# Router on the residual rows, two prefetched parts behind the first gather, and GpSimd adding the returned rows of two tiles, in a hybrid encoder with a mixture of experts

## The chip, the cores and the metric

The kernel runs on one core of a Trainium2 chip. The metric is the device time of one execution in microseconds (us). PE is TensorE, DVE is VectorE, ACT is ScalarE, POOL is GpSimd, and SP is SyncE, which here only issues DMAs.

## The reference

One encoder layer on 512 tokens of 1024 float32 values: a token mixer (windowed attention and gated linear attention, merged and added to the input), then a mixture of experts, then a last RMS norm. The change touches what follows the token mixer.

```python
hn = rms_norm(x, norm_ffn[l])
x = x + hier_moe(hn, ...)
return rms_norm(x, norm_final)

# hier_moe, for each token
g_logits = xt @ w_rg + b_rg                      # 4 groups, the best is taken
e_logits = xt @ w_re + b_re                      # 32 experts, the 2 best of that group are taken
top_w = softmax(top_v) * g_w                     # the weights of the 2 experts
h = silu(xt @ w_gate[e]) * (xt @ w_up[e])        # 1024 -> 256
out = out + (h * weight) @ w_down[e]             # 256 -> 1024
```

`rms_norm(x, g)` is `x * rsqrt(mean(x*x) + 1e-6) * g`. A row's factor is a scalar, so a router logit is also `factor * (x @ (g * w)) + b`.

## The kernel before

The 512 tokens are four tiles of 128 rows (tile t holds tokens 128t to 128t+127). The residual rows stand in `x2`, the normed rows in `hn_st`; `hn_dram` is the copy of the normed rows in HBM from which rows are gathered.

**Routing** lies between the mixer and the experts. For each tile: `residual(t)` adds the mixer's output (DVE), `row_squares(t)` (ACT) and two POOL instructions make the row factor `rstd2`, `normed(t)` (DVE) writes `hn_st`, `turn_hn(t)` (PE) transposes it by eight matmuls, `turned_rows` (ACT) and `router_in` (DVE) copy the halves out of PSUM, `route` (PE) multiplies them by the router weights `rw`, `turned_logits` (ACT) and `token_major` (PE) bring the logits back to one row for each token, and `router_out` (DVE) adds the bias. Then DVE finds group and experts in a chain of small instructions, each of which waits for the one before (`link`), writes the one-hot choice `selb`, PE counts ranks with it, and DVE turns ranks into the number of the slot that each of the two choices of a token takes (`pf`). From `pf` DVE builds eight one-hot matrices `hot[:, k, 0, :]`, and PE multiplies each by `first_in` (`keep_busy` puts a dummy matmul behind most of them). The result is `gcolm`, the tokens of the first two pairs of experts, for which the first two gathers wait.

**Experts.** The 32 experts are 16 pairs of 64 slots each. `first_gather(0)` and `first_gather(1)` (POOL, DMA queue 0) fetch the rows of pairs 0 and 1; later gathers and scatters go through the same queue. The weights come in 96 parts of 1 MB (pair, matrix, expert) through SP's queue (queue 1), which is a list written out by hand. A ring holds R = 21 parts. The first 21 are prefetched; part 21 and those behind wait until PE has used a part (`used`), the first of them for half of the gate matrix of pair 0. Parts 11 and 20 are the last ones prefetched: SP waits for the router's last matmul (`rl_done` 6), issues part 11, waits for the rows of `hn_dram` and for the transposes, and issues part 20.

**Tail.** The first 14 pairs write their weighted rows through HBM (`z_dram`); once all are written (`moe_done`), SP loads them back as `zt`, two rows for each token. For tiles 0 and 1 DVE adds both rows to `x2` (`final_add`), for tiles 2 and 3 PE adds them into PSUM (`rows_to_tokens`). Pairs 14 and 15 don't go through HBM: ACT and DVE split their output in two parts (`last_high`, `last_low`), and PE brings them to token order (`to_tokens`). DVE adds the PSUM banks to `x2` (`final_acc`), ACT and POOL make the last row factors, DVE scales (`final_norm`), and SP stores.

Of the kernel before, what the change touches and what calls it, by code (L numbers as in the profile page):

```python
# [8 lines left out]
F32 = mybir.dt.float32  # L9
# [4 lines left out]
ALU = mybir.AluOpType  # L14
# [4 lines left out]
P = 128  # L19
# [90 lines left out]
def hybrid_encoder(nc, x, w_in, rel_bias, attn_sink, wr_f, br_f, wr_b, br_b, gla_norm, w_a, w_b, w_out,  # L110
# [7 lines left out]
    with ctx:  # L118
# [13 lines left out]
        gcol = sb("gcol", [P, KC])  # L132
# [72 lines left out]
        g8 = startup[0:KC, 1536:1536 + P]  # L205
# [80 lines left out]
        ZERO_PIECES = 2 * NT  # L286
        arrived = {(n_, m_): sum(32 if q_ in HALVED else 16 for q_, (p_, w_, _) in enumerate(order)
# [142 lines left out]
        def _(sp):  # L430
# [169 lines left out]
        def _(pool):  # L600
# [78 lines left out]
            first_gather(0)  # L679
            first_gather(1)  # L680
# [28 lines left out]
            pool.sem_inc(s["moe_done"], 1)  # L709
            for t in range(NT):  # L710
# [5 lines left out]
        def _(pe):  # L716
# [16 lines left out]
            pe.wait_ge(s["norm_in"], 16)  # L733
            tr(bank[KC - 1][:, 0:KC], g8).then_inc(s["gc_done"], 1)
# [289 lines left out]
            def turn_hn(t):  # L1024
                pe.wait_ge(s["hn_done"], t + 1)
                for c in range(KC):
                    ins = tr(bank[2 * t + c // 4][:, (c % 4) * P:(c % 4 + 1) * P], hn_st[:, t, c * P:(c + 1) * P])
                    if c % 4 == 3:
                        ins.then_inc(s["hT_done"], 1)

            def route(t0, t1):
                pe.wait_ge(s["hnT_outA"], t1)
# [27 lines left out]

            pe.wait_ge(s["cb_done"], 5)
# [4 lines left out]
            keep_busy(22)  # L1066
# [12 lines left out]
            for k in range(2 * NT):  # L1079
                pe.wait_ge(s["hot_done"], k + 1)  # L1080
                ins = mm(bank[6][:, 0:2], hot[:, k, 0, :], first_in[:, k, :], start=(k == 0), stop=(k == 2 * NT - 1))
                if k < 2 * NT - 1:
                    keep_busy(1)
            ins.then_inc(s["first_done"], 1)
            for k in range(2 * NT):
                pe.wait_ge(s["hot_done"], 2 * NT + k + 1)
# [5 lines left out]
            def slot_weights():  # L1092
                pe.wait_ge(s["gcolm_done"], 1)
                for k in range(2 * NT):
                    pe.wait_ge(s["hot_done"], 4 * NT + k + 1)
# [170 lines left out]
        def _(act):  # L1266
# [8 lines left out]
            act.dma_start(g8, norm_mix.rearrange("(c p) -> c p", p=P)).then_inc(s["norm_in"], 16)  # L1275
# [8 lines left out]
            A(gcol[:], bank[KC - 1][:, 0:KC], ACT.Copy).then_inc(s["gcol_done"], 1)  # L1284
# [891 lines left out]
```

## Time and profile before

| | us |
|---|---|
| median of 3 runs (623.71, 623.91, 625.61) | 623.91 |
| the profiled execution | 623.14 |
| its span, first to last instruction | 621.4 |
| PE busy | 584.4 (94%) |
| DVE busy | 268.0 (43%) |
| ACT busy | 209.2 (34%) |
| POOL busy | 65.6 (11%) |
| DMA, mean rate | 251 GB/s |

The busy shares are means over stages that differ: the routing lies between about 352 and 388 us, the pairs of experts between 388 and 600 us, the tail behind them. A busy PE is not a PE at its peak, and dummy matmuls count as busy.

### The profile page before, as it was taken

To read this page: it belongs to the slowest core of one execution; us is meant where nothing else is said; L and a number is where in the kernel's file an instruction comes from. 1 tells how busy PE (TensorE), PEld (TensorE's weight loads), DVE (VectorE), ACT (ScalarE), POOL (GpSimd) and SP (SyncE) were. 2 spreads that over 40 slices of the span, in tenths; PEclk is the share of its full clock that TensorE was granted. 3 is DMA by queue.
4 is the path that set the end of the run, shared out by engine and by line. 5 is a ranking of instruction groups with operands and counts; after the bars stand their busy time and mean duration, and the time that the engine had idled before them with its cause. 6 is when DMAs were issued, how large, how long until landed. Compare 5 with 4: busy or idle time off the path is not lost.

```text
span 621.4 us, 8693 instructions
## 1 busy us (share of the span) xinstructions
PE 584.4 (94%) x3453; PEld 443.0 (71%) x3454; DVE 268.0 (43%) x590; ACT 209.2 (34%) x407; POOL 65.6 (11%) x108
## 2 busy tenths in 40 slices
PE   3999999999999999999999998999999998887894
PEld 3789989888688888888888874766666765553451
DVE  3647477654433657433362377312111211012247
ACT  3545466554596633422252240111111111111113
POOL 4000000000002201100000012112212211111001
PEclk9999999999999999999999999999999999889998
DMA  7476030802222222188888288899999999999994
GB/s 252 91 257 201 7 103 10 302 37 69 68 78 59 68 69 69 35 278 282 298 318 347 102 315 328 321 401 424 422 423 426 421 423 426 426 423 425 425 422 183
DMA packets 58282, 155.83 MB, mean 251 GB/s; under 512 B 8172, under 2 KB 38148, under 8 KB 45952
## 3 DMA queue, kind: packets, MB, share of 16 engines
q1 hardware_dynamic: 53392, 145.73, 61.4%
q0 software_dynamic: 4720, 9.45, 4.1%
q8 instruction: 28, 0.46, 0.3%
q14 instruction: 14, 0.11, 0.1%
q10 hardware_dynamic: 128, 0.09, 0.0%
HBM read 147.37 MB, written 15.75 MB: 263 GB/s over the span
## 4 chain that ended last, share of the span: by engine, by line
PE 76%; DMA 11%; SPq 5%; DVE 5%; issue 1%; POOL 1%; ACT 1%; DVEq 0%; POOLq 0%; ACTq 0%
PE bank L728 43%; PE bank L1118 11%; PE bank L1139 6%; PE bank L721 5%; SPq L492 5%; DMA slot2a<-expert_w_up 5%; DMA zt<-expert_rows 3%; PE bank L823 1%; DMA expert_rows<-y,zcol 1%; PE bank L904 1%; DMA x_in<-x 1%; PE bank L801 1%; PE bank L802 1%; PE bank L927 1%; PE bank L883 1%
## 5 line engine op out<-in xcount | busy, mean ns | idle before, releaser
L1118 PE MATMUL bank<-slots,xgT 128*64 128x256 f32 x544 | 79.9, 388 | 4.8 <-DMA slot2b<-expert_w_up 2.4
L1723 DVE TENSOR_TENSOR w_low<-w,w_high 128x1024 fp32r<-128x1024 f32 x32 | 39.2, 1225 | 75.5 <-ACT w_high L1368 75.5
L1118 PEld LDWEIGHTS bank<-slots,xgT 128*64 128x64 f32 x544 | 53.7, 139 | 22.4 <-issue 4.6
L728 PE MATMUL bank<-x_high,w_high 128*128 128x512 f32 x168 | 67.0, 399 | 1.0 <-DVE x_low L1640 1.0
L728 PE MATMUL bank<-x_high,w_low 128*128 128x512 f32 x168 | 65.6, 391 | 0.0
L728 PE MATMUL bank<-x_low,w_high 128*128 128x512 f32 x168 | 65.6, 390 | 0.0
L1368 ACT ACTIVATE w_high<-w 128x1024 fp32r<-128x1024 f32 x32 | 33.7, 1054 | 48.7 <-PE bank L728 48.7
L2013 DVE TENSOR_SCALAR y<-bank,slot_weights 128x512 f32<-128x512 f32 x14 | 10.5, 751 | 86.6 <-PE bank L1139 86.6
L728 PE MATMUL bank<-w_high,x_high 128*128 128x420 f32 x128 | 45.4, 354 | 0.0
L728 PE MATMUL bank<-w_high,x_low 128*128 128x420 f32 x128 | 45.3, 354 | 0.0
L728 PE MATMUL bank<-w_low,x_high 128*128 128x420 f32 x128 | 45.2, 353 | 0.0
L728 PEld LDWEIGHTS bank<-x_high,w_high 128*128 128x128 f32 x168 | 31.6, 188 | 9.2 <-issue 1.6
L1532 ACT ACTIVATE y<-bank,slot_weights 128x512 f32<-128x512 f32 x14 | 9.6, 687 | 80.5 <-PE bank L1139 80.5
L728 PEld LDWEIGHTS bank<-x_high,w_low 128*128 128x128 f32 x168 | 31.5, 188 | 6.8
L728 PEld LDWEIGHTS bank<-x_low,w_high 128*128 128x128 f32 x168 | 31.6, 188 | 6.3
L1118 PE MATMUL bank<-slot2b,xgT 128*64 128x256 f32 x192 | 30.9, 391 | 0.0
L1526 ACT ACTIVATE h_silu<-bank 128x256 f32<-128x256 f32 x14 | 5.4, 384 | 74.7 <-PE bank L1118 74.7
L1693 DVE CUSTOM_DVE_ANT_0 s_sb<-bank,bias,sink 128x256 f32<-128x256 f32 (+1 forms) x32 | 17.6, 549 | 29.4 <-PE bank L802 29.4
L2003 DVE TENSOR_TENSOR h_sb<-h_silu,bank 128x256 f32<-128x256 f32 x14 | 5.9, 421 | 53.9 <-ACT h_silu L1526 53.9
L1139 PE MATMUL bank<-slots,hT 128*64 128x512 f32 x112 | 25.5, 593 | 1.7 <-issue 1.7
L1294 ACT ACTIVATE w_high<-w 128x512 fp32r<-128x512 f32 (+1 forms) x18 | 18.8, 1069 | 19.0 <-DMA w<-w_in 14.2
L728 PE MATMUL bank<-w_high,merged_high 128*128 128x512 f32 x64 | 24.9, 389 | 0.0
(279 smaller groups left out, 1150.0 us busy)
## 6 DMA issues: line engine op xcount, KB each, us to landing
slots<-expert_w_gate SPq DMA_DIRECT2D x19, 1024.0 KB, 28.1
slots<-expert_w_up SPq DMA_DIRECT2D x17, 1024.0 KB, 20.5
slots<-expert_w_down SPq DMA_DIRECT2D x16, 1024.0 KB, 8.0
slot2b<-expert_w_down SPq DMA_DIRECT2D x9, 1024.0 KB, 27.3
w<-w_in SPq DMA_DIRECT2D x16, 512.0 KB, 3.7
slot2b<-expert_w_up SPq DMA_DIRECT2D x8, 1024.0 KB, 8.2
slot2b<-expert_w_gate SPq DMA_DIRECT2D x8, 1024.0 KB, 28.3
w<-w_in SPq DMA_DIRECT2D x8, 840.0 KB, 4.7
```

The costliest lines, as they stand in the source:

```text
L492: sp.dma_start(ring[q % R], (g_rows, u_rows, d_rows)[m][:, 2 * pair + e, :]).then_inc(m_in[pair % 4][m], 16)
L721: return nc.tensor.transpose(out_, in_, K["ident"][0:n, 0:n])
L728: ins_ = mm(out_, stat[a_], mov[b_], start=first and q_ == 0, stop=last and q_ == 2)
L801: mm(out_, q2[:, h, qs], kh[:, kv, ks], start=True, stop=False)
L1118: ins = mm(bank[2][e * SLOTS:(e + 1) * SLOTS, m * FE:(m + 1) * FE], xgT[:, c, e * SLOTS:(e + 1) * SLOTS], gu[m][e][:, c], start=(c == 0), ...
L1139: ins = mm(bank[4 + f][e * SLOTS:(e + 1) * SLOTS, :], hT[:, j, e * SLOTS:(e + 1) * SLOTS], dn[e][:, j, f * 512:(f + 1) * 512], start=(j == ...
L1294: ins_ = A(h, raw, ACT.Copy)
L1368: A(wh2[:, u % 2, :], raw2[:, u % 2, :], ACT.Copy).then_inc(s["hi_done"], 1)
L1532: A(y_sb[k][:, 0:512], bank[4][:, :], ACT.Copy, scale=weight).then_inc(s["y_outA"], 1)
L1693: V.tensor_tensor_reduce(s_sb[:, i % 2, 0:n], bank[i % 2][:, 0:n], bias[:, h, band], 1.0, sink[:, h:h + 1], ALU.add, ALU.max, mx[:, i % 2: ...
L1723: V.tensor_tensor(wl2[:, u % 2, :], raw2[:, u % 2, :], wh2[:, u % 2, :].bitcast(F32), ALU.subtract).then_inc(s["lo_done"], 1)
L2013: V.tensor_scalar(y_sb[k][:, 512:1024], bank[5][:, :], weight, None, ALU.mult).then_inc(s["y_outD"], 1)
```

## The change

1. The router works on residual rows. PE transposes `x2` instead of `hn_st` (`turn_x2`), the gain `norm_ffn` is multiplied into the router weights once, early (`gate_weights`; it arrives by one more small DMA beside `norm_mix`), and `router_out` multiplies by the row factor `rstd2`. `normed(2)` and `normed(3)` now stand behind copies of the router's input on DVE, and ACT's `row_squares(3)` behind all four `turned_rows`.
2. The choice `selb` is made from the sum of the two small one-hots; the two large ones (`sel`) follow behind it.
3. The eight one-hot matrices are made by three instructions (4, 3 and 1 matrices) from a reordered copy of the constants made at the start, and `first_in` by two. PE's dummy matmuls between the eight products are gone, and 22 dummies before `selb` are 19.
4. Parts 11 and 20 are issued when POOL has passed `first_gather(0)` and raised `pool_step`.
5. In the tail POOL adds the two returned rows of tiles 0 and 1, DVE's `final_add` is one instruction for each tile, and the order on DVE is new.

```diff
@@ SP
             sp.wait_ge(s["rl_done"], 6)
-            load_part(11)
             sp.wait_ge(s["hn_out"], 16 * (ZERO_PIECES + NT))
             sp.wait_ge(s["hT_done"], 2 * NT)
+            sp.wait_ge(s["pool_step"], 1)
+            load_part(11)
             load_part(20)
@@ POOL
             first_gather(0)
+            pool.sem_inc(s["pool_step"], 1)
             first_gather(1)
...
             pool.sem_inc(s["moe_done"], 1)
+            for t in range(2):
+                pool.wait_ge(s[f"rows_in{t}"], 32)
+                nc.gpsimd.tensor_tensor(zt[:, t, 0, :], zt[:, t, 0, :], zt[:, t, 1, :], ALU.add).then_inc(s["f_add"], 1)
@@ PE
-            def turn_hn(t):
-                pe.wait_ge(s["hn_done"], t + 1)
+            def turn_x2(t):
+                pe.wait_ge(s["x2_done"], 2 * (t + 1))
...
-            for t in range(3):
-                turn_hn(t)
+            for t in range(NT):
+                turn_x2(t)
             route(0, 2)
-            turn_hn(3)
+            route(2, 3)
             token_major(0, 2, 1)
-            route(2, 3)
             route(3, 4)
...
-            keep_busy(22)
+            keep_busy(19)
...
             for k in range(2 * NT):
-                pe.wait_ge(s["hot_done"], k + 1)
+                pe.wait_ge(s["hot_done"], 1 + sum(k >= k0 for k0 in HOT_CUTS[:-1]))
                 ins = mm(bank[6][:, 0:2], hot[:, k, 0, :], first_in[:, k, :], start=(k == 0), stop=(k == 2 * NT - 1))
-                if k < 2 * NT - 1:
-                    keep_busy(1)
@@ ACT
             for t in range(3):
                 row_squares(t)
-            turned_rows(0)
+            for t in range(NT):
+                turned_rows(t)
             row_squares(3)
@@ DVE
+            V.tensor_copy(dealt.rearrange("p (x e l) -> p x e l", l=4, e=8), K["iota"].rearrange("p (x l e) -> p x e l", l=4, e=8)
...
+                V.tensor_tensor(rw[:], rw[:], bc(gcol_ffn, NG + EXPERTS), ALU.mult).then_inc(s["cb_done"], 1)
...
-            for k in range(2 * NT):
-                V.tensor_scalar(hot[:, k, 0, :].rearrange("p (x e l) -> p x e l", l=4, e=8), dealt, pf[:, 0, k:k + 1], None, ALU.is_equal)
...
+            for k0, k1 in zip((0,) + HOT_CUTS, HOT_CUTS):
+                V.tensor_tensor(hot[:, k0:k1, 0, :], dealt.unsqueeze(1).to_broadcast([P, k1 - k0, P]), bc(pf[:, 0, k0:k1], P),
+                                ALU.is_equal).then_inc(s["hot_done"], 1)
@@ DVE, tail
-            final_add(0, 0)
-            final_add(0, 1)
             last_low(1, 0)
-            final_add(1, 0)
+            first_rows = final_add(0)
             last_low(1, 1)
-            final_add(1, 1)
-            for t in range(NT):
-                final_acc(t)
+            dve.wait_ge(s["dve_step"], first_rows)
+            final_acc(0)
+            dve.wait_ge(s["dve_step"], final_add(1))
+            final_acc(1)
+            final_acc(2)
             dve.wait_ge(s["gain_in"], 32)
-            for t in range(NT):
+            final_norm(0)
+            final_acc(3)
+            for t in range(1, NT):
                 final_norm(t)
```

Three places in the order of instructions follow. The first is PE between the mixer's last product and the ranks. `hn_st` is the normed row and `x` the residual row (`x2`), `hnT` the transposed router input, L1046 and L1052 are `token_major`. Before:

```order
L721 MATMUL bank<-cst,hn_st 128x128 x24
L1037 MATMUL bank<-hnT,rw 36x256 x8
L721 MATMUL bank<-cst,hn_st 128x128 x8
L1046 MATMUL bank<-both_halves,turned_logits 128x36 x2
L1037 MATMUL bank<-hnT,rw 36x128 x16
L1046 MATMUL bank<-both_halves,turned_logits 128x36 x2
```

And in the changed kernel:

```order
L728 MATMUL bank<-cst,x 128x128 x32
L1045 MATMUL bank<-hnT,rw 36x256 x8
L1045 MATMUL bank<-hnT,rw 36x128 x8
L1052 MATMUL bank<-both_halves,turned_logits 128x36 x2
L1045 MATMUL bank<-hnT,rw 36x128 x8
L1052 MATMUL bank<-both_halves,turned_logits 128x36 x2
```

All 32 transposes stand in one piece ahead of the router's products, and none of them reads a normed row.

The second is DVE behind the slot numbers `pf`. Before, a row of `hot` and one of `first_tokens_in` (`first_in`) alternate eight times (the first two turns are shown):

```order
L1979 CAST pf<-pi 128x8
L1983 TENSOR_SCALAR hot<-cst,pf 128x128
L1984 TENSOR_SCALAR first_tokens_in<-cst,pf 128x2
L1983 TENSOR_SCALAR hot<-cst,pf 128x128
L1984 TENSOR_SCALAR first_tokens_in<-cst,pf 128x2
```

In the changed kernel the whole stretch up to `gcolm` is:

```order
L1987 CAST pf<-pi 128x8
L1989 TENSOR_TENSOR first_tokens_in<-cst,pf 128x16
L1991 TENSOR_TENSOR first_tokens_in<-first_tokens_in,cst 128x16
L1994 TENSOR_TENSOR hot<-cst,pf 128x4x128
L1994 TENSOR_TENSOR hot<-cst,pf 128x3x128
L1994 TENSOR_TENSOR hot<-cst,pf 128x128
L1998 TENSOR_SCALAR gcolm<-bank 128x2
```

Sixteen instructions became five.

The third is the end of DVE's list, with the semaphores that each row waits for (`ylast` is `last_low`, `x<-x,zt` is `final_add`, `x<-x,bank` is `final_acc`, the last ones are `final_norm`). In the changed kernel:

```order
L2101 SCALAR_TENSOR_TENSOR ylast<-bank,slot_weights,ylast 128x512 [waits ly_hi]
L2129 TENSOR_TENSOR x<-x,zt 128x1024 [waits f_acc,f_add]
L2101 SCALAR_TENSOR_TENSOR ylast<-bank,slot_weights,ylast 128x512 [waits ly_hi]
L2107 TENSOR_TENSOR x<-x,bank 128x512 [waits comb_done,dve_step]
L2107 TENSOR_TENSOR x<-x,bank 128x512 [waits comb_done]
L2129 TENSOR_TENSOR x<-x,zt 128x1024 [waits f_acc,f_add]
L2107 TENSOR_TENSOR x<-x,bank 128x512 [waits comb_done,dve_step]
L2107 TENSOR_TENSOR x<-x,bank 128x512 [waits comb_done] x3
L2137 SCALAR_TENSOR_TENSOR x<-x,row_norms,gfin 128x1024 [waits rstd_done,gain_in]
L2107 TENSOR_TENSOR x<-x,bank 128x512 [waits comb_done] x2
L2137 SCALAR_TENSOR_TENSOR x<-x,row_norms,gfin 128x1024 [waits rstd_done] x3
```

The first `last_low` now stands ahead of every `final_add`, and the second behind one `final_add` of one instruction, which waits for POOL's sum (`f_add`).

## Rows read from the trace of the kernel before

**Rows 1.** The page, part 2: 40 slices of 15.5 us each
```profile
GB/s 252 91 257 201 7 103 10 302 37 69 68 78 59 68 69 69 35 278 282 298 318 347 102 315 328 321 401 424 422 423 426 421 423 426 426 423 425 425 422 183
```

**Rows 2.** Busy time by stage, with granted clock, DMA share and GB/s
```profile
core 0: us, PE busy (x) PEld busy (x) DVE busy (x) ACT busy (x) POOL busy (x), PEclk, DMA share, GB/s
382.00:384.00 2.00, 1.64 (x12) 1.33 (x13) 2.00 (x9) 0.00 (x0) 1.00 (x1) 1.00 0.74 311
...
388.00:390.00 2.00, 2.00 (x20) 1.62 (x22) 1.82 (x9) 1.14 (x1) 1.02 (x1) 1.00 0.04 10
480.00:500.00 20.00, 20.00 (x153) 13.54 (x151) 3.64 (x7) 2.71 (x6) 4.08 (x7) 1.00 1.01 424
```

**Rows 3.** Chain of waits, 355 to 392 us: start, us, what
```profile
362.56 0.67 PE bank L721 x4
...
369.86 0.24 DVE lg L1914
...
375.05 0.30 DVE selb L1963
...
377.95 0.33 DVE hot L1983
...
381.89 0.17 DVE gcolm L1988
...
382.75 0.03 POOLq L674
...
383.00 3.46 DMA xg<-hn_rows,gcolm
```

**Rows 4.** Timeline, 355 to 425 us: start, us, engine, line, operation
```profile
360.15 1.91 PE L721 MATMUL bank<-cst,hn_st 128*128 128x128 f32 x16
...
363.85 1.92 PE L1037 MATMUL bank<-hnT,rw 128*36 128x256 f32 x16 [0.20 <-ACT hnT L1496]
...
364.92 0.32 SPq L540 DMA_DIRECT2D hn_rows<-hn_st  x1
...
372.44 0.34 SPq L492 DMA_DIRECT2D slot2d<-expert_w_up  x1
372.47 1.85 POOL L647 MEMSET xg<- 128x1024 f32 x2 [9.07 <-DMA hn_rows<-hn_st]
```

**Rows 5.** Timeline of SP's queue: the first load after the prefetch
```profile
389.96 0.33 SPq L505 DMA_DIRECT2D slots<-expert_w_up  x1
```

**Rows 6.** The page, part 5: VectorE, both inputs in SBUF
```profile
L1723 DVE TENSOR_TENSOR w_low<-w,w_high 128x1024 fp32r<-128x1024 f32 x32 | 39.2, 1225 | 75.5 <-ACT w_high L1368 75.5
```

**Rows 7.** The tile xg: the 16 gathers, issue to landing
```profile
DMA to landing us min/median/max: 3.5/8.0/9.2
```

**Rows 8.** DMA of 384.5:385 us, queue 0: packets, MB, share of 16 engines
```profile
q0 software_dynamic: 6, 0.02, 26.1%
```

**Rows 9.** DMA of 391.5:392 us, queue 1: packets, MB, share of 16 engines
```profile
q1 hardware_dynamic: 28, 0.11, 69.1%
```

**Rows 10.** Line 635 on GpSimd: duration ns min/median/max
```profile
L635 POOL TENSOR_TENSOR kend<-kend,tok x8: 731/741/1007, 189.2 to 215.3; 128x256 f32<-128x256 f32 x8
```

**Rows 11.** Timeline of the tail, 578 to 621 us
```profile
601.51 2.48 DVE L2122 TENSOR_TENSOR x<-x,zt 128x1024 f32<-128x1024 f32 x2 [1.66 <-DMA zt<-expert_rows]
...
603.92 0.74 DVE L2091 SCALAR_TENSOR_TENSOR ylast<-bank,slot_weights,ylast 128x512 fp32r<-128x512 f32 x1
603.95 0.69 ACT L1576 ACTIVATE ylast<-bank,slot_weights 128x512 fp32r<-128x512 f32 x1 [1.03 <-PE bank L1213]
...
604.81 4.27 PE L1220 MATMUL bank<-ylast,owner 128*128 128x512 f32 x16 [0.90 <-DVE ylast L2091]
605.71 0.75 DVE L2091 SCALAR_TENSOR_TENSOR ylast<-bank,slot_weights,ylast 128x512 fp32r<-128x512 f32 x1
...
609.01 3.65 PE L1226 MATMUL bank<-zt,two_rows 128*64 128x512 f32 x16
...
613.32 4.87 DVE L2132 SCALAR_TENSOR_TENSOR x<-x,row_norms,gfin 128x1024 f32<-128x1024 f32 x4
```

More of the change, by code:

```diff
@@ L1273, in step @@
                 return steps[0]
-            act.dma_start(g8, norm_mix.rearrange("(c p) -> c p", p=P)).then_inc(s["norm_in"], 16)
+            for half_, gains in enumerate((norm_mix, norm_ffn)):
+                act.dma_start(g16[half_ * KC:(half_ + 1) * KC, :], gains.rearrange("(c p) -> c p", p=P)).then_inc(s["norm_in"], 16)
             act.dma_start(onehot, c_onehot).then_inc(s["onehot_in"], 16)
@@ L1283, in _ @@
             act.wait_ge(s["gc_done"], 1)
-            A(gcol[:], bank[KC - 1][:, 0:KC], ACT.Copy).then_inc(s["gcol_done"], 1)
+            A(gcols[:], bank[KC - 1][:, 0:2 * KC], ACT.Copy).then_inc(s["gcol_done"], 1)
             def split_high(k):
@@ L1678, in _ @@
             V.memset(unit_base, UNIT).then_inc(s["cb_done"], 1)
+            dve.wait_ge(s["cb_done"], 4)
+            dealt = K["before"]
+            V.tensor_copy(dealt.rearrange("p (x e l) -> p x e l", l=4, e=8), K["iota"].rearrange("p (x l e) -> p x e l", l=4, e=8)
+                          ).then_inc(s["cb_done"], 1)
             def maxima(i):
@@ L1913, in router_out @@
                 dve.wait_ge(s["rl_done"], turned)
-                V.tensor_tensor(lg[:, t0:t1, :], bank[1 + t0][:, t0 * (NG + EXPERTS):t1 * (NG + EXPERTS)].rearrange(
-                    "p (t n) -> p t n", n=NG + EXPERTS), rb[:].unsqueeze(1).to_broadcast([P, t1 - t0, NG + EXPERTS]), ALU.add
-                    ).then_inc(s["rl_out"], 1)
+                for t in range(t0, t1):
+                    V.scalar_tensor_tensor(out=lg[:, t, :], in0=bank[1 + t0][:, t * (NG + EXPERTS):(t + 1) * (NG + EXPERTS)],
+                                           scalar=rstd2[:, t:t + 1], in1=rb[:], op0=ALU.mult, op1=ALU.add).then_inc(s["rl_out"], 1)
             residual(0)
@@ L1923, in _ @@
             residual(3)
-            normed(2)
             router_in(0)
             router_in(1)
-            normed(3)
+            normed(2)
             router_in(2)
             router_in(3)
-            router_out(0, 2, 2)
+            normed(3)
+            router_out(0, 2, 3)
             router_out(2, 4, 6)
-            dve.wait_ge(s["rl_out"], 2)
+            dve.wait_ge(s["rl_out"], NT)
             g_lg = lg[:, :, 0:NG]
@@ L1958, in _ @@
             V.tensor_tensor(ex, v2, v1, ALU.subtract).then_inc(s["rexp_in"], 1)
+            link(V.tensor_tensor(tmp8, hot1, hot2, ALU.add))
+            by_group = "p t (g i) -> p t g i"
+            V.tensor_tensor(selb[:].rearrange(by_group, g=NG), bc(g_hot, NE), tmp8.unsqueeze(2).to_broadcast([P, NT, NG, NE]),
+                            ALU.mult).then_inc(s["selb_done"], 1)
             for k, oh in enumerate((hot1, hot2)):
-                ins = V.tensor_tensor(sel[:, k].rearrange("p t (g i) -> p t g i", g=NG), bc(g_hot, NE),
+                ins = V.tensor_tensor(sel[:, k].rearrange(by_group, g=NG), bc(g_hot, NE),
                                       oh.unsqueeze(2).to_broadcast([P, NT, NG, NE]), ALU.mult)
             link(ins)
-            V.tensor_tensor(selb[:], sel[:, 0], sel[:, 1], ALU.add).then_inc(s["selb_done"], 1)
             dve.wait_ge(s["rank_done"], 1)
@@ L2114, in _, with final_add @@
             last_turned(1)
-            def final_add(t, w):
-                if w == 0:
-                    dve.wait_ge(s[f"rows_in{t}"], 32)
-                    dve.wait_ge(s["f_acc"], NT)
-                else:
-                    dve.wait_ge(s["f_add"], 2 * t + 1)
-                V.tensor_tensor(x2[:, t, :], x2[:, t, :], zt[:, t, w, :], ALU.add).then_inc(s["f_add"], 1)
+            def final_add(t):
+                dve.wait_ge(s["f_add"], t + 1)
+                dve.wait_ge(s["f_acc"], NT)
+                return step(V.tensor_tensor(x2[:, t, :], x2[:, t, :], zt[:, t, 0, :], ALU.add))
             def final_acc(t):
-                if t < 2:
-                    dve.wait_ge(s["f_add"], 2 * t + 2)
                 for f in range(2):
```

32 lines of the change are left out of this document (15 added, 17 removed).

## Prediction

> **What bounds the kernel now.** I read the rates by slice first. From the 27th slice (about 404 us) to the last but one the chip moves 401 to 426 GB/s, flat, while the slices before it swing [rows 1]. So the end of the kernel is set by DMA: whatever is still to be moved when the stream starts is moved at one rate, and PE, though busy throughout 480 to 500 us, only rides on it [rows 2]. A microsecond saved in PE's or DVE's work behind 404 us is worth nothing by itself; what counts is when the stream starts, and what lies behind it in the tail.
>
> The start is the next thing to look at. The prefetch ends a little after 383 us: the rate is 311 GB/s at 382 to 384 and 10 GB/s at 388 to 390, when SP has nothing it may issue [rows 2]. The next load goes out at 389.96 [rows 5], when PE has used half a gate matrix of pair 0. That load hangs on gather 0, which is issued at 383.00 and lands 3.46 us later, and the gather hangs on a chain that runs through PE's transposes, the logits, the choice, the one-hots and `gcolm` [rows 3]. So the routing chain is on the path, one microsecond for one microsecond, down to the start of the stream.
>
> **The change part by part, the router.** PE transposes 16 blocks in 1.91 us [rows 4], then waits until 362.56 for the normed row of tile 2 [rows 3], and the transposes of tile 3 come later still. In the new order 32 transposes run in one piece from 360.15 to 364.0, twice the 1.91; they need only `x2` of tile 3. Then `route(0, 2)` takes 1.92 us for two tiles [rows 4], so 3.84 us for four, and one pair of `token_major` about 0.3 us: 368.1. Before, the last `token_major` let DVE go on at 369.86 [rows 3]; I trace the last copies at the same lengths (about 0.8 us) and get 368.9, a gain of 1.0 us. `router_out` has two instructions behind the last wait where there was one, about 0.1 us. Net 0.9.
>
> **The choice.** Two instructions (0.41 us together) and one of 0.30 before `selb` become a small one of about 0.2 and one of 0.3; `selb` was ready at 375.35 [rows 3]. Gain 0.2. The two large ones hide behind PE's rank count, which lasts as long as they do; without that cover they cost 0.4 again.
>
> **The one-hots.** From 377.95 to 381.89, 3.94 us, DVE and PE alternate eight times [rows 3]. The new stretch has two small instructions (0.3 us with the wait between them) and 1024 elements for each partition in three pieces. DVE takes 1225 ns for 1024 with two inputs in SBUF [rows 6], and three pieces instead of one add some 0.1. Then one more matmul and its wait, 0.3. Sum 1.9, gain 2.0. PE's eight products run under the pieces.
>
> Routing together: 0.9 + 0.2 + 2.0 = **3.1 us**; gather 0 would go out at 379.9 instead of 383.00.
>
> **The parts behind the gather.** Without parts 11 and 20 (2.1 MB, 4.9 us at 424 GB/s) SP's queue is empty some 5 us sooner, at about 378.4, so at 379.9 nothing is ahead of the gather. But where does POOL raise `pool_step`? The trace has POOL's queue at the second gather's register move at 382.75, and the first gather's own descriptor work only begins at 383.00 [rows 3]. The queue runs ahead of the engine, and the new signal stands between the two. So I take it that SP is let go about 0.2 us before the gather starts, not behind it. From SP's issue (389.96) to real bytes on queue 1 (the half microsecond to 392) is 1.6 us [rows 5, 9]; from the gather's start (383.00) to its first bytes (the half microsecond to 385) about as long [rows 3, 8]. Parts and gather then start together and share the engines. What that costs has two ends: nothing (3.5 us, the fastest gather), and the price in the full stream, where the median gather takes 8.0 us, 4.5 more [rows 7]. Two parts are a short burst, 4.9 us, and not a queue that stays full, and the gather's first bytes are not far behind theirs. I take a third of the upper end, **1.5 us**, nearer to the idle row since nothing stands in the queue ahead of the parts. That moves the start of the stream from 389.96 to about 388.4, and parts 11 and 20, needed by pairs 2 and 3, have landed by then, so no bytes are carried over. A page says more simply how queues share: by the Trainium skill, DMA: Bandwidth & Descriptors, § Queues, rings and completion order, an engine takes turns between its queues packet by packet. With equal turns the gather's own 1.2 us of data would take 2.4, a delay of 1.2 and not 4.5; the gathers of the stream do not agree with it.
>
> **Stores of the normed rows.** `normed(3)` waits for `row_squares(3)` behind four copies, so the last store leaves at about 367.6 instead of 364.92 [rows 4], and parts 10, 18 and 19 behind it on SP. POOL's clearing of `xg`, 1.85 us from 372.47 [rows 4], waits for that store. Before, the store took 7.5 us with parts around it; the same again ends the clearing at 377, 2.9 us ahead of the gather. Cost nothing; if that cover were gone, one for one.
>
> **Edits at the start.** A reordered copy (0.3 us, like one `hot` of 0.33 [rows 3]), a product over 288 elements (0.4 us at the rate of [rows 6]) and a DMA of 4 KB. DVE is busy 43%, PE's products cover them. Uncovered, 0.8 us.
>
> **The tail.** POOL has never added 128x1024 here. Its 128x256 product took 741 ns, at worst 1007 [rows 10]. Four times that is 3.0 us; if 0.2 of the 741 is fixed, 2.4. Bounds: 2.4, and 4.0 from the worst row. The rows of tile 0 land at 601.51 [rows 11]. Sum at 604.2 (2.7 us), `final_add(0)` to 605.4 (1.22), `last_low(1, 1)` to 606.2, where it ended at 606.46 before. Its input from ACT was ready at 604.64; so before, too, DVE kept it back. PE starts its products about 1 us sooner, since the first `last_low` no longer waits behind two adds (603.92), but the fourth tile's product needs the second `last_low`, and the sixteen matmuls and the 3.65 us behind them end about 0.3 sooner [rows 11]. DVE does 2.4 us less, one `final_norm` moves ahead of the last `final_acc`, but three norms (3.7 of the 4.87 us) still stand behind it. I take **0.3 us**, between 0.6 (POOL 2.4) and a loss of 1.0 (POOL 4.0).
>
> **Sum.** 3.1 - 1.5 + 0.3 = 1.9 us off the profiled execution of 623.14 (span 621.4, 1.7 around it). The median of the runs, 623.91, is 0.8 above it; I take the difference off the median: **622.0**. 0.3% is 1.9 us, about what a measurement tells from no change: so "faster" means below 622.0, and the forecast lies on that border.
>
> **Rivals.**
> - *The gather is not delayed.* If the signal comes behind the gather's 1.2 us, or short bursts don't hurt it, the delay is at most 0.3: 3.1 - 0.2 + 0.3 = 3.2 gained, **620.7**. For it: the two start together, and nothing was queued. Against it: the queue that runs ahead. 27%.
> - *The gather is delayed as in the stream, and the kernel is no faster or slower.* 4.5 us of delay: 3.1 - 4.5 + 0.3 = -1.1, **625.0**. The place is gather 0 behind parts 11 and 20; it decides from a delay of 3.4 us, a landing 6.9 us from issue. For it: 14 gathers around 8.0. Against it: the burst has drained some 6.5 us after the gather's start. At the slowest row, 9.2, it would be 5.7 of delay and 626.2. 17%.
> - *The adds on POOL are late.* 4.0 us each: the second `last_low` ends 1.0 later, and PE and the norms with it. 3.1 - 1.5 - 1.0 = 0.6, **623.3**. A page speaks for it: the Trainium skill, GPSIMD Engine Reference, § Key points, has POOL contend with VectorE instructions that have two inputs in SBUF, which `final_add(0)` is while POOL makes its second sum. 12%.
> - *The clock falls.* PE now idles between the last of the eleven dummies and the eight products. If the granted clock went to 1.2 GHz there, the 3.5 us between landing and first load [rows 3, 5] would at most double: about 3 us lost, **625**. The clock is 1.00 in each of these stretches [rows 2], and the new gaps are of about 2 us. 4%.
>
> The forecast itself has 40%.
>
> **From cases to numbers.** Of the forecast's 40% a little over half lies below 622.0, and nearly all of the first rival: faster 0.50. The late adds, the rest of the forecast and most of the delayed gather are within 0.3%: 0.41. The slowest gathers and the clock: 0.09. The range reaches from 619.8 (no delay, POOL at its best, a little more from the one-hots) to 624.0 (delay of 3.5).
>
> **What would show it.** In the profile after: DVE's first logits instruction ends its wait at about 368.9; from `pf` to `gcolm` about 2.0 us; gather 0 issued near 379.9; SP's part 11 issued no later than the gather's start (if it comes 1.2 us later, the reading of POOL's queue is wrong); the gather's landing 5.0 us from its issue; the first load behind the prefetch near 388.4; flat 424 GB/s from then on. In the tail: POOL's sums of 2.4 to 3.0 us, the second `last_low` ending 4.7 us behind the landing of tile 0's rows. The prediction fails if the gather lands in under 4 or over 7 us, if POOL takes over 3.5 us, or if the stream's end does not follow its start.

## The result, and the profile after

The changed kernel takes 632.29 us (median of 4 runs, 631.40 to 633.52), the kernel before 623.81 on the same chip (4 runs): ratio 1.013, 95% interval 1.0113 to 1.0147. It is 1.3% slower. The forecast of 622.0 and its range, up to 624.0, missed it, and so did every rival.

The routing did what was expected of it. The chain of waits after (start, us, what), against [rows 3]:

```profile
370.18 0.43 DVE lg L1920 x2
...
375.24 0.30 DVE selb L1966
...
378.20 0.18 DVE first_tokens_in L1989
...
380.35 0.17 DVE gcolm L1998
...
381.45 8.51 DMA xg<-hn_rows,gcolm
...
390.00 1.97 PE bank L728 x8
```

The gather is issued 1.55 us earlier. The last row is what went wrong: it took 8.51 us where it had taken 3.46. What SP issued around it (timeline of SP's queue):

```profile
359.00 2.72 SPq L542 DMA_DIRECT2D hn_rows<-hn_st  x2
...
381.32 0.34 SPq L494 DMA_DIRECT2D slot2c<-expert_w_gate  x1
381.69 0.43 SPq L494 DMA_DIRECT2D slot2d<-expert_w_up  x1
...
395.63 0.33 SPq L507 DMA_DIRECT2D slots<-expert_w_up  x1
```

The second and third rows are parts 11 and 20, 1 MB each; the last is the first load behind the prefetch, 5.67 us later than in [rows 5]. The first row is the store of normed rows 0 and 1. It left at 357.75 before; here, 1.25 us later, before any edited instruction of the routing can matter. Kernels below whose code is that of before up to there show it at 358.3 to 359.3, and those with the changed start at 357.7 to 359.4, so I take it for the scatter of single executions and not for an effect of the change. Busy time by stage (columns as in [rows 2]):

```profile
core 0: us, PE busy (x) PEld busy (x) DVE busy (x) ACT busy (x) POOL busy (x), PEclk, DMA share, GB/s
380.00:382.00 2.00, 1.49 (x11) 1.27 (x12) 1.65 (x8) 0.00 (x0) 0.55 (x1) 1.00 0.20 86
382.00:384.00 2.00, 2.00 (x10) 1.24 (x9) 0.66 (x3) 0.00 (x0) 1.66 (x2) 0.51 0.74 205
384.00:386.00 2.00, 2.00 (x9) 0.72 (x7) 0.52 (x2) 0.00 (x0) 0.00 (x0) 0.64 1.04 438
386.00:388.00 2.00, 0.36 (x2) 0.00 (x0) 0.00 (x0) 0.00 (x0) 0.00 (x0) 1.00 0.99 414
388.00:390.00 2.00, 0.00 (x0) 0.00 (x1) 0.00 (x0) 0.00 (x0) 0.00 (x0) 0.72 0.66 254
390.00:392.00 2.00, 2.00 (x10) 1.67 (x12) 0.00 (x0) 0.82 (x2) 0.00 (x0) 0.50 0.00 0
392.00:394.00 2.00, 2.00 (x10) 1.14 (x12) 1.81 (x8) 1.05 (x1) 1.02 (x2) 0.50 0.03 8
440.00:500.00 60.00, 60.00 (x452) 40.45 (x452) 10.98 (x21) 8.43 (x16) 12.06 (x20) 1.00 1.02 417
500.00:560.00 60.00, 50.47 (x372) 30.85 (x373) 9.78 (x18) 6.81 (x13) 10.43 (x18) 1.00 1.02 418
```

Three things are to be seen here. The engines move the burst from 384 to about 389 at full rate, and the gather's rows land when it is over. Then TensorE, idle since about 386.4, works at 0.50 of its clock, the 1.2 GHz level: eight transposes take 1.97 us instead of 1.15, and landing to first load takes 5.67 us instead of 3.5. And the stream runs at 417 and 418 GB/s, where the kernel before had 423 and 424: that was on nobody's list. The two rows of before:

```profile
386.50 1.15 PE L721 MATMUL bank<-cst,xg 128*128 128x128 f32 x8 [0.24 <-DMA xg<-hn_rows,gcolm]
...
440.00:500.00 60.00, 60.00 (x452) 40.36 (x450) 10.97 (x20) 8.40 (x16) 12.07 (x20) 1.00 1.01 423
```

The DMA view can be asked for each queue by itself. MB moved in each microsecond of the changed kernel, queue 1 (SP's loads) and queue 0 (the two gathers, issued at 381.45 and right behind):

| from | 382 | 383 | 384 | 385 | 386 | 387 | 388 | 389 |
|---|---|---|---|---|---|---|---|---|
| queue 1 | 0.12 | 0.29 | 0.45 | 0.43 | 0.29 | 0.32 | 0.20 | 0.00 |
| queue 0 | 0 | 0 | 0 | 0 | 0.10 | 0.11 | 0.18 | 0.13 |

Queue 0's first bytes come in 386:386.5, some 4.6 us after the gather's issue. In e3 below, with nothing beside it, they come 1.6 us after. From 386 on the two queues share the engines.

The tail (timeline), against [rows 11]:

```profile
610.35 5.89 POOL L716 TENSOR_TENSOR zt<-zt 128x1024 f32<-128x1024 f32 x2 [28.33 <-DMA zt<-expert_rows]
...
612.77 1.23 DVE L2129 TENSOR_TENSOR x<-x,zt 128x1024 f32<-128x1024 f32 x1 [0.96 <-POOL zt L716]
613.91 0.75 DVE L2101 SCALAR_TENSOR_TENSOR ylast<-bank,slot_weights,ylast 128x512 fp32r<-128x512 f32 x1
...
617.21 3.65 PE L1227 MATMUL bank<-zt,two_rows 128*64 128x512 f32 x16
```

From the landing of tile 0's rows to the end of the span it takes 19.5 us (629.8 - 610.3) instead of 19.9.

The difference of the two profiled spans, 629.8 - 621.4 = 8.4 us, comes apart at three points: the first load is 5.67 later, the stretch from it to the returned rows lasts 214.7 instead of 211.6 (+3.1), and the tail is 0.4 shorter. The 5.67 are +1.25 (scatter at the start), -2.8 (routing: 1.55 and that scatter), +5.05 (gather), +2.2 (from landing to load).

### The profile page after: what moved, and what is told of

It is laid out like the page before. It is cut to its first block, busy times and chain, and to the rows that moved or that the text cites. A ratio compares the mean times of both kernels' runs of the same rounds, so it can differ in the third digit from the quotient of the medians.

```text
span 629.8 us, 8668 instructions
## 1 busy us (share of the span) xinstructions
PE 581.8 (92%) x3441; PEld 439.3 (70%) x3444; DVE 264.4 (42%) x582; ACT 209.4 (33%) x407; POOL 72.1 (11%) x110
## 2 busy tenths in 40 slices
DMA packets 58298, 155.83 MB, mean 247 GB/s; under 512 B 8181, under 2 KB 38165, under 8 KB 45969
## 4 chain that ended last, share of the span: by engine, by line
PE 70%; DMA 14%; SPq 7%; DVE 4%; issue 2%; POOL 1%; ACT 1%; POOLq 0%; ACTq 0%; DVEq 0%
PE bank L735 38%; PE bank L1119 12%; SPq L494 6%; PE bank L728 5%; PE bank L1140 5%; DMA slot2a<-expert_w_up 5%; DMA zt<-expert_rows 3%; DMA w<-w_in 2%; PE bank L830 1%; DMA xg<-hn_rows,gcolm 1%; DMA expert_rows<-y,zcol 1%; SPq L447 1%; PE bank L911 1%; DMA x_in<-x 1%; PE bank L808 1%
## 5 line engine op out<-in xcount | busy, mean ns | idle before, releaser
L1119 PE MATMUL bank<-slots,xgT 128*64 128x256 f32 x544 | 78.5, 389 | 4.6 <-DMA slot2b<-expert_w_up 2.3
L1119 PEld LDWEIGHTS bank<-slots,xgT 128*64 128x64 f32 x544 | 51.5, 140 | 24.0 <-issue 4.4
L1119 PE MATMUL bank<-slot2b,xgT 128*64 128x256 f32 x192 | 29.2, 381 | 0.4 <-DMA slot2b<-expert_w_gate 0.4
L735 PEld LDWEIGHTS bank<-w_high,x_high 128*128 128x128 f32 x128 | 24.0, 188 | 1.3 <-DVE w_low L1631 0.9
```

The costliest lines, as they stand in the source:

```text
L735: ins_ = mm(out_, stat[a_], mov[b_], start=first and q_ == 0, stop=last and q_ == 2)
L1119: ins = mm(bank[2][e * SLOTS:(e + 1) * SLOTS, m * FE:(m + 1) * FE], xgT[:, c, e * SLOTS:(e + 1) * SLOTS], gu[m][e][:, c], start=(c == 0), ...
```

## The experiments

Four theories. **A**: the burst beside the gather holds it back, and the wait leaves TensorE at its lower clock. **B**, its rival in the first four runs: the loss is the slower stream and the later start, from other edits. **C**, formed after those four runs: the stream is slower because of 32 bytes of SBUF. Its rival **D**: something else in the routing edit slows the stream. One table holds the readings of every kernel: gather 0's issue and time (chain of waits), from its landing to the first load and that load (SP's queue), from the load to tile 0's returned rows, the rate in 440:500, the median, the kernel before on the same chip, and the ratio.

| kernel | issue, time | to load | load | stream | GB/s | us | before | ratio, 95% |
|---|---|---|---|---|---|---|---|---|
| before | 383.00, 3.46 | 3.5 | 389.96 | 211.6 | 423 | 623.81 | | |
| changed | 381.45, 8.51 | 5.7 | 395.63 | 214.7 | 417 | 632.29 | 623.81 | 1.0130 (1.0113-1.0147) |
| e1_parts_back | 381.63, 7.49 | 3.5 | 392.63 | 215.0 | 417 | 629.11 | 624.14 | 1.0074 (1.0048-1.0100) |
| e2_parts_alone | 383.65, 8.41 | 5.7 | 397.73 | 211.4 | 423 | 630.94 | 624.14 | 1.0098 (1.0063-1.0134) |
| e3_behind_landing | 381.45, 3.38 | 3.5 | 388.34 | 216.5 | 417 | 626.50 | 624.14 | 1.0039 (1.0022-1.0056) |
| e4_tail_alone | 383.92, 3.41 | 3.5 | 390.85 | 211.4 | 424 | 623.51 | 624.14 | 0.9989 (0.9967-1.0012) |
| e5_pad_alone | 384.00, 3.45 | 3.5 | 390.96 | 214.0 | 417 | 627.58 | 624.63 | 1.0049 (1.0031-1.0068) |
| e6_realigned | 380.49, 3.43 | 3.5 | 387.43 | 213.8 | 424 | 624.09 | 624.63 | 0.9997 (0.9978-1.0016) |
| e7_clock_held | 382.52, 9.17 | 4.9 | 396.64 | 214.0 | 417 | 632.76 | 624.63 | 1.0135 (1.0100-1.0170) |
| e8_one_part_early | 381.04, 4.4 | 3.7 | 389.12 | 210.9 | 423 | 623.37 | 624.63 | 0.9978 (0.9957-0.9999) |
| e9_clock_held_longer | 382.46, 9.36 | 3.5 | 395.33 | 214.4 | 417 | 631.57 | 624.44 | 1.0112 (1.0095-1.0128) |
| e10_pad_64_bytes | 383.56, 3.36 | 3.5 | 390.43 | 213.7 | 418 | 627.40 | 624.44 | 1.0054 (1.0037-1.0071) |
| e11_one_part_burst | 380.19, 7.61 | 4.9 | 392.74 | 211.6 | 423 | 627.26 | 624.44 | 1.0052 (1.0035-1.0069) |
| e12_changed_realigned | 382.12, 8.97 | 4.9 | 396.04 | 211.4 | 423 | 628.08 | 624.44 | 1.0044 (1.0024-1.0065) |
| e13_pad_128_bytes | 384.47, 3.47 | 3.5 | 391.45 | 214.1 | 418 | 627.49 | 624.58 | 1.0047 (1.0030-1.0064) |

In e8 the landing is read from SP's issue of part 20, which waits for it. Absolute times carry the scatter at the start (up to 1.7 us); times between two points don't.

### The gather: e1, e2, e3, e4, e11

**e1_parts_back** is the changed kernel with the SP order of before.

```diff
             sp.wait_ge(s["rl_done"], 6)
+            load_part(11)
             sp.wait_ge(s["hn_out"], 16 * (ZERO_PIECES + NT))
             sp.wait_ge(s["hT_done"], 2 * NT)
-            sp.wait_ge(s["pool_step"], 1)
-            load_part(11)
             load_part(20)
```

> The changed kernel with part 4 undone (parts 11 and 20 issued early again, as before). Theory A (the two parts hold gather 0 back by 5 us, and PE's clock falls in the wait): of the 8.4 us lost, gather and clock make 7.2; but now the prefetch itself drains until about 385 us beside a gather issued near 381.5, so part of the delay stays. Landing 5 to 7 us from issue, clock 1.00, 625 to 628 us. Theory B (the loss is the slower stream, 417 against 424 GB/s, and the later start of the mixer, both from other edits): the gather matters little, 629 us or more.

Measured: 629.11 us, parts issued at 371.42 and 375.54, and the gather still took 7.49 us.

```profile
380.00:382.00 2.00, 1.49 (x10) 1.21 (x9) 1.50 (x8) 0.00 (x0) 0.37 (x1) 0.74 1.05 442
382.00:384.00 2.00, 2.00 (x9) 1.27 (x7) 0.84 (x3) 0.00 (x0) 1.70 (x2) 0.50 1.02 430
384.00:386.00 2.00, 2.00 (x12) 1.17 (x11) 0.52 (x2) 0.00 (x0) 0.14 (x1) 0.90 0.97 399
386.00:388.00 2.00, 0.50 (x3) 0.00 (x1) 0.00 (x0) 0.00 (x0) 0.00 (x0) 1.00 0.52 197
```

These windows of e1 say why: at 381.63, when the gather is issued, the prefetch is not over. By queue, it moves 0.39 to 0.46 MB in each microsecond to 385, 0.22 in the next and 0.06 in the one behind; 1.7 MB in all are moved between the gather's issue and its landing at 389.1. In the kernel before, the prefetch ran dry at 383.4 and the gather was issued at 383.0: its 3.46 us are those of a gather that meets a queue which is just empty. So routing made faster by 2.8 us gains nothing if the parts stay: the gather only waits longer. The prefetch even ends later in e1: the last normed row is stored 3.8 us later (368.73 for 364.92, 1.4 of it the scatter), SP waits 3.6 us for it instead of 2.2, and part 20 goes out at 375.54 instead of 372.44.

The time and the delay came out just outside what A had expected (625 to 628 us, 5 to 7 us), the clock was not 1.00 throughout but 0.50 in 382:384, and 629 us was B's number. Both had a part in it: the first load is 2.7 us later than before, and the stream is 3.4 longer.

**e2_parts_alone** is the reverse: the kernel before with part 4 of the change and nothing else.

```diff
-            load_part(11)
             sp.wait_ge(s["hn_out"], 16 * (ZERO_PIECES + NT))
             sp.wait_ge(s["hT_done"], 2 * NT)
+            sp.wait_ge(s["pool_step"], 1)
+            load_part(11)
             load_part(20)
@@ POOL
             first_gather(0)
+            pool.sem_inc(s["pool_step"], 1)
```

> The kernel before with part 4 alone. Theory A: gather 0, issued at 383.0, lands 8.5 us later instead of 3.5, the clock falls, 623.8 + 5.0 + 2.2 = 631 us. Theory B: nothing but the order of two loads changed, 624 us.

Measured: 630.94, a gather of 8.41 us, a clock of 0.50 behind it (392:396), and the stream at 423 GB/s. Theory B had 624. The new place of the two parts alone costs 6.8 us, with the old routing and with dummies between the products.

**e3_behind_landing** is the changed kernel with the parts behind the rows themselves.

```diff
-            sp.wait_ge(s["pool_step"], 1)
+            sp.wait_ge(s["gathered0"], 16)
             load_part(11)
             load_part(20)
```

> The changed kernel, parts 11 and 20 issued when gather 0 has landed instead of when it has been issued. Theory A: gather 0 lands 3.5 us after issue, the clock stays at 1.00, the start of the stream moves 7.2 us forward against the changed kernel, about 1.5 us of bytes of the two parts are carried into the stream: 632.3 - 7.2 + 1.5 = 626.5, and 623.5 if the slower stream was part of the same disturbance. Theory B: 629 or more.

Measured: 626.5, gather 3.38 us, clock 1.00 throughout 380:400:

```profile
381.45 3.38 DMA xg<-hn_rows,gcolm
```

Against the changed kernel one wait takes 5.8 us away, and the first load is at 388.34. By 5.13 us of gather and 2.2 of clock it should have been 7.3 less; the rest is that most of the two parts' 2.1 MB now move behind the first load: the stream is 216.5 us long, 1.7 more. It is still 0.4% slower than before, though its first load is 1.6 us sooner; that, and 417 GB/s, is what led to C.

**e4_tail_alone** is the kernel before with the changed tail (part 5) alone.

```diff
@@ POOL
+            for t in range(2):
+                pool.wait_ge(s[f"rows_in{t}"], 32)
+                nc.gpsimd.tensor_tensor(zt[:, t, 0, :], zt[:, t, 0, :], zt[:, t, 1, :], ALU.add).then_inc(s["f_add"], 1)
@@ DVE
-            final_add(0, 0)
-            final_add(0, 1)
             last_low(1, 0)
-            final_add(1, 0)
+            first_rows = final_add(0)
             last_low(1, 1)
...
```

> The kernel before with part 5 alone (POOL adds the returned rows of tiles 0 and 1, new order on DVE). From the trace of the changed kernel the tail behind the landing of tile 0's rows took 19.5 us where it took 19.9: 0.4 us less, 623.4. If the tail edit is what slows the stream (theory B), 626 or more.

Measured: 623.51 against 624.14, ratio 0.9989 (0.9967 to 1.0012). No change can be told, and the sign fits the 0.4 us of the tail.

**e11_one_part_burst** asks for the size: e8 (below), but part 20 goes out at the gather's start and not at its landing, so 1 MB instead of 2 stands beside the gather.

```diff
             sp.wait_ge(s["rl_done"], 6)
             load_part(11)
...
-            sp.wait_ge(s["gathered0"], 16)
+            sp.wait_ge(s["pool_step"], 1)
             load_part(20)
```

> e8_one_part_early with part 20 issued at gather 0's start (as in the changed kernel) and not behind its landing: 1 MB instead of 2 MB is issued beside the gather. Theory A as the runs so far size it: the gather waits for nearly all bytes issued beside it; 2.10 MB at 424 GB/s are 4.95 us, and it took 8.5 instead of 3.5. So 1.05 MB give 2.5 us: landing 6.0 us after the issue, and a time 1 to 2 us above e8_one_part_early, near 625. Rival (the queues share by packet, the delay comes from something else in part 11's place): 4.5 us or less.

Measured: 7.61 us, and 627.26, 3.9 above e8: more than the 6.0 us that the bytes of part 20 alone give. So what counts is not what is issued beside the gather but all that is outstanding then, the tail of the earlier parts too: queue 1 moves 1.49 MB between the gather's issue and its landing, part 20's 1.05 and 0.44 of parts issued before. The rival (4.5 us or less) falls.

One sum fits the sizes, as an estimate: 3.46 us, the gather of before, and the MB that queue 1 moved between issue and landing, at 424 GB/s.

| kernel | queue 1, MB | sum, us | measured |
|---|---|---|---|
| e11 | 1.49 | 7.0 | 7.61 |
| e1 | 1.70 | 7.5 | 7.49 |
| e2 | 2.10 | 8.4 | 8.41 |
| changed | 2.12 | 8.5 | 8.51 |
| e7 | 2.10 | 8.4 | 9.17 |
| e12 | 2.15 | 8.5 | 8.97 |
| e9 | 2.10 | 8.4 | 9.36 |

It is met within 0.1 us three times and is 0.4 to 1.0 short four times. Why those four take longer is open. In e11 each queue moves at most 0.03 MB in any half microsecond from 385.5 to the landing at 387.8, so the last bytes come long after the rate has dropped.

### The clock: e7 and e9

Both are the changed kernel with dummies back on PE, e7 with 24 behind the tables and e9 with 34.

```diff
                 ins = mm(bank[6][:, 0:2], hot[:, k, 0, :], first_in[:, k, :], start=(k == 0), stop=(k == 2 * NT - 1))
+                if k < 2 * NT - 1:
+                    keep_busy(1)
...
-            keep_busy(7)
+            keep_busy(34)
```

> The changed kernel with TensorE's dummies put back: one between each two of the eight products of the one-hot table, and 24 behind the tables instead of 7. Theory A's second half (the granted clock fell to half because TensorE was left idle around the gather, and the first tiles ran at half speed): the clock stays at 1.00 in 380:400, landing of gather 0 to first load behind the prefetch takes about 3.5 us instead of 5.67, the gather itself takes 8.5 us as before, the time is about 630 us. Rival (the late first tiles cost nothing beyond the gather's own delay, or the clock falls while TensorE waits whatever the dummies do): 632 us.

Measured: 632.76. The clock was 1.00 to 392, but the dummies ended at 389.45, TensorE was idle 2.28 us, and it fell (0.69 in 392:394, then 0.50 in 394:396). Landing to load took 4.9 us, and the dummies between the products put the gather 1.07 later. The time is the rival's 632 and not the 630 expected; but the clock was not held, so this decides nothing. Hence e9:

> e7_clock_held with 34 dummies behind the tables instead of 24: there they ended at 389.45, TensorE stood idle until gather 0's rows at 391.73, and the clock fell after all (0.50 at 394:396; 4.9 us from the landing to the first load behind the prefetch). With 34 they end at 391.7, as the rows land. Theory A's second half: the clock stays at 1.00 to 398, and the landing to the first load takes 3.4 to 3.5 us instead of 5.67 in the changed kernel; gather 0 itself still takes 8.5 to 9.2. The dummies between the products put the gather 1.1 us later, so the time is about 631 us. Rival (the clock falls at that place whatever TensorE does): 4.9 us or more to the first load, 632.5 us.

Measured: 631.57; windows of e9 and its first load:

```profile
390.00:392.00 2.00, 1.64 (x8) 0.63 (x7) 0.00 (x0) 0.00 (x0) 0.00 (x0) 1.00 0.22 84
392.00:394.00 2.00, 1.67 (x14) 1.41 (x16) 0.90 (x3) 1.37 (x2) 0.18 (x1) 1.00 0.00 0
...
395.33 0.33 SPq L507 DMA_DIRECT2D slots<-expert_w_up  x1
```

The clock stays at 1.00, and landing to load is 3.5 us: the 2.2 us are the clock's. As a cure it is worth little, since its own dummies cost 1.0 and the gather stayed at 9.36 us.

### The 32 bytes: e5, e10, e13, e6, e12

The routing edit replaces `gcol`, eight columns, by `gcols`, sixteen. Everything allocated behind it lies 32 bytes further; the ring's first slot moves from byte 48,640 of a partition (95 x 512) to 48,672. **e5_pad_alone** is the kernel before with this and not one instruction changed:

```diff
-        gcol = sb("gcol", [P, KC])
+        gcol = sb("gcol", [P, 2 * KC])[:, 0:KC]
```

> The kernel before with one edit: gcol is allocated 16 wide instead of 8, so that everything allocated after it in SBUF lies 32 bytes further (the ring's first slot at byte 48,672 of a partition instead of 48,640); no instruction changes. Theory C (the 32 bytes slow the stream of weights): the windows 440:500 and 500:560 move 417 to 419 GB/s instead of 423 to 425, and the time is about 627 us (+3). Rival D (something else in the routing edit slows the stream): 424 GB/s and 624 us.

Measured: 627.58 against 624.63, ratio 1.0049 (1.0031 to 1.0068), and in 440:500:

```profile
440.00:500.00 60.00, 60.00 (x454) 40.49 (x452) 10.97 (x20) 8.34 (x15) 12.07 (x20) 1.00 1.02 417
```

The engines are as busy as before (share 1.02 for 1.01) and move 1.4% less. D falls. **e10_pad_64_bytes** and **e13_pad_128_bytes** allocate 24 and 40 columns.

```diff
-        gcol = sb("gcol", [P, KC])
+        gcol = sb("gcol", [P, 3 * KC])[:, 0:KC]
```

> The kernel before with gcol allocated 24 wide: everything behind it lies 64 bytes further, the ring begins at byte 48,704, a multiple of 64 and no longer of 512. If what counts is a boundary of 64 bytes: 423 to 425 GB/s in 440:500 and 624 us, as before. If it is a larger boundary (512, as the address of before has): 417 to 419 GB/s and 627 us, as e5_pad_alone.

> The kernel before with gcol allocated 40 wide: everything behind it lies 128 bytes further, the ring begins at byte 48,768, a multiple of 128 and no longer of 256 or 512. If a boundary of 128 bytes is what counts: 423 to 425 GB/s in 440:500 and about 624.5 us. If it is 256 or 512: 417 to 419 GB/s and 627.5 us, as with 32 and 64 bytes.

Measured: 418 GB/s and 627.4, 418 GB/s and 627.49. A multiple of 64 or 128 is not enough.

Must it be 512? A pad of 256 was not run, but the kernels at 423 to 424 GB/s answer it by themselves. Not every part of their ring lies at a multiple of 512: 15 of the 21 do, and the other six (five in `slot2b`, from byte 188,160, and `slot2d`, at 163,584) lie at a multiple of 256 only. The loads go round the ring in order, so queue 1's bytes, counted from the first load, tell when the five parts of `slot2b` are written. In before that is about 467.6 to 479.8 and 526.1 to 537.7, and the rate there is 424 and 424 GB/s, with 423 to 425 in the stretches into `slots01` around them. Over the seven kernels with these addresses the stretches into `slot2b` run at 421 to 425, those into `slots01` at 420 to 426. So 256 is enough here. In the eight kernels that are shifted by 32, 64 or 128 bytes no such stretch is above 422, and all fifteen traces fall on the side of their address.

Queue 1 carries nothing but loads into the ring in 440:500. It takes the same 90.4% of the engines' time in before and in e5, and moves 22.89 MB there and 22.53 here: it is these loads that are slower, by 1.6% for each byte. By what step they lose it no trace shows.

**e6_realigned** is e3 with the addresses of before, **e12_changed_realigned** the changed kernel with them:

```diff
-        gcols = sb("gcols", [P, 2 * KC])
+        sb("gcol", [P, KC])
...
         lg = sb("lg", [P, NT, NG + EXPERTS])
+        gcols = lg[:, 0, 0:2 * KC]
```

> e3_behind_landing with its addresses put back: the 16 columns of gcols lie inside lg, which is free until the routing, and 32 unused bytes stand where gcol stood, so that the ring begins at byte 48,640 again. Theory C: the stream is back at 423 to 425 GB/s and the time is 623.5 us, 3 below e3_behind_landing. Rival D: 417 to 419 GB/s and 626.5 us again.

> The changed kernel with nothing but its addresses put back as in e6_realigned. Theory C, if it is additive: 423 to 425 GB/s in 440:500, gather 0 still 8.5 us, and about 629.3 us (3 below the changed kernel). Rival (behind a late start of the stream the rate of the stream hides): 632 us.

Measured: e6 624.09, 424 GB/s; e12 628.08, 423 GB/s, with a gather of 8.97 us. On e3 the addresses are worth 2.4 us and 2.6 of stream (216.5 to 213.8), on the changed kernel 4.2 and 3.3. So the cost of the addresses stands beside the gather's and is not hidden by it; the difference between 2.4 and 4.2 is not much more than the spread of the medians.

### The version that uses the whole change: e8

e6 has the first load 2.5 us before that of the kernel before and is no faster, because its stream is 2.3 us longer: the two parts move there, and the DMA engines stood nearly idle ahead of the landing (37 GB/s in 380:382). **e8_one_part_early** gives them one part to do.

```diff
             sp.wait_ge(s["rl_done"], 6)
+            load_part(11)
             sp.wait_ge(s["hn_out"], 16 * (ZERO_PIECES + NT))
             sp.wait_ge(s["hT_done"], 2 * NT)
             sp.wait_ge(s["gathered0"], 16)
-            load_part(11)
             load_part(20)
```

> e6_realigned with part 11 issued at its place of before (behind the free of its slot, near 371 us) and part 20 alone behind gather 0's landing. The DMA engines, idle at 380 to 383 us in e3_behind_landing, have part 11's bytes to move ahead of gather 0. If part 11 is over when gather 0 starts: gather 0 in 3.5 us, first load at 388.4, and the time is 621 to 622 us, below the kernel before by about 2. If part 11 still delays it: the time is that of e6_realigned or more.

Measured: 623.37 against 624.63, ratio 0.9978 (0.9957 to 0.9999), the fastest of all. Its windows:

```profile
380.00:382.00 2.00, 1.60 (x9) 1.26 (x9) 2.00 (x9) 0.00 (x0) 0.96 (x1) 0.76 0.71 299
382.00:384.00 2.00, 2.00 (x8) 1.22 (x7) 0.25 (x1) 0.00 (x0) 1.24 (x2) 0.50 0.52 156
384.00:386.00 2.00, 2.00 (x12) 1.10 (x11) 0.52 (x2) 0.00 (x0) 0.00 (x0) 0.88 0.59 168
```

The prefetch runs dry at about 381.4 where the gather is issued at 381.04, the same meeting as in the kernel before, some 2 us sooner. It is 0.2% faster; by the bound of 0.3% that is hardly told from no change, and it is less than was expected (621 to 622).

The trace has a reason, and it isn't the stream. Tile 0's rows return 1.2 us sooner than in e6, but the end of the span comes 21.8 us behind them, where every other kernel takes 19.4 to 20.0:

```profile
600.04 4.83 POOL L716 TENSOR_TENSOR zt<-zt 128x1024 f32<-128x1024 f32 x2 [27.32 <-DMA zt<-expert_rows]
...
604.09 1.85 DVE L2129 TENSOR_TENSOR x<-x,zt 128x1024 f32<-128x1024 f32 x1
```

DVE's `final_add(0)` starts 1.7 us behind POOL's sum, since it stands behind the first `last_low`, and that waits for the last pairs. PE reaches the first product of pair 15 at 591.28, e6 at 590.03. Before it, PE waits 2.57 us for a load of `expert_w_up` (2.03 in e6), the granted clock falls (0.76 in 578:580, 0.50 in 580:582), and the 32 products behind take 5.36 us instead of 3.67. So in this execution the chain that ends last goes through PE. That the clock stayed up in the four of ten executions at 621.1 to 622.2 would fit, but is not shown; only one execution was profiled, at 623.86.

## Why the prediction was wrong

- **What bounds the kernel**: right in the main. In the pads and in e6 and e12 the span follows the first load and the stream; e8's one trace is an exception, where PE's own work at the lower clock ended last.
- **Router** (0.9 forecast): 0.9. DVE's logits ended their wait at 370.18; less the 1.25 of scatter that is 368.9, as worked out. **Choice** (0.2): 0.1. **One-hots** (2.0): 1.8. Routing 2.8 for 3.1: right.
- **The parts behind the gather**: the step that failed. That POOL's signal comes ahead of the gather's own work was right (part 11 at 381.32, the gather at 381.45). "I take a third of the upper end, 1.5 us" was wrong: it cost 5.05 here, 4.95 in e2, above even the end taken from the full stream (4.5). The argument in its favour, a short burst and nothing ahead of the parts, misread the case. The gather is late by about the time of the outstanding bytes: 2.1 MB at 424 GB/s are 4.9 us. The sentence held against the slower rival, that the burst has drained some 6.5 us after the gather's start, pointed at the mechanism. The sum with 5.05 in this place gives 625.6; e12, without the 32 bytes, is at 628.1, with 1.4 of the rest from the clock, 0.5 from a still later gather and 0.5 from the kernel before on its chip (624.44 for 623.91). One reading was wrong besides: a gather moves 0.27 MB and not 0.5 (queue 0 moves 0.27 MB in e3 up to the first landing, 0.52 for both gathers), so its own data are 0.6 us and not 1.2. The packet-by-packet turns of the Trainium skill, DMA: Bandwidth & Descriptors, § Queues, rings and completion order, would with equal turns have given a delay of 0.6, as an estimate from that. Sharing is seen in the changed kernel from 386 on, but not in the 3 us before it, in which only queue 1 moved; no gather beside a burst shows so small a delay.
- **The clock** (4%): it fell, and cost 2.2 to the first load. The rival had it fall in the 2 us gap ahead of the products, from rows where the gather landed in time. It was the gather's own delay that made the long gap; the two were not separate cases with separate chances. Of the late gathers those of the changed kernel, e2, e7, e11 and e12 brought the fall, after 2.3 to 5.2 us of idle TensorE; e9, kept busy, did not, and neither did e1, after 2.67.
- **The term that was missing**: 3 us for 32 bytes. Nothing in the prediction asked what a wider tile does to the addresses behind it. "Flat 424 GB/s from then on" was the sign that showed it.
- **The tail** (0.3): 0.4 in the profile. POOL's first sum took 2.4 us, the low end (610.35 to `final_add(0)` at 612.77); the second took 3.4, beside DVE's `final_add(0)`. So the contention that the rival of the late adds named is there: in e8, where the add started 1.7 us later and met only the last 0.8 us of the second sum, both sums took 2.37 and the add 1.85 instead of 1.23. It cost the tail little: in the changed kernel `final_add(1)` starts at 616.55, 0.3 us behind the second sum. The second `last_low` ended 4.4 us behind the landing, forecast 4.7.
- **The normed rows' stores and the edits at the start**: nothing, as forecast. The clearing of `xg` ended at 377.1, forecast 377.

## What to carry to other kernels

Before a transfer is moved next to a latency-critical one, count the bytes outstanding when the critical one is issued, and take their whole time as its delay (it was that, or up to 1 us more, in each of the seven cases here); put the bulk so that it runs dry just then, or behind the landing. A faster chain ahead of such a transfer gains only if the bulk ends earlier too. And when a small tile grows, look at the addresses of the large DMA targets behind it, which did best here at multiples of 256 bytes, and compare the rate of a flat stretch before and after.

## What was not expected of the hardware

- Moving the SBUF tiles by 32, 64 or 128 bytes off a multiple of 256 cost 1.2 to 1.4% of the stream's rate (417 to 418 for 423 to 424 GB/s), with no change in instructions, bytes or packets (58,282 packets and 155.83 MB in before and in e5).
- A gather of 0.27 MB in its own queue, issued 0.1 us behind the start of a burst of 2.1 MB in another, took 8.4 to 9.4 us; alone 3.4 to 3.5.
- The granted clock fell in e7 after 2.28 us of idle TensorE and in e8 (at 578) after 2.57, and did not in e1 after 2.67. In the changed kernel, e1, e8 and e12 it also fell to about 0.5 for 2 to 4 us from 381 or 382 on, among the tables' matmuls, and in e3, e6 and e11, whose PE code is the same, it did not. Idle time alone does not say when; that stays open.
- The same code reaches the mixer's end up to 1.5 us apart from execution to execution (store of normed row 0 at 357.75 to 359.25 in kernels that are equal up to there). Spans of single profiles are therefore compared from a common point.
